# Encoder layer (attention, DeltaNet, experts): q, k, v projection of the DeltaNet as seven products of halves

## Chip, cores and metric

The kernel runs on one core of a Trainium2 chip. The metric is the device time of one execution in microseconds (us), the median over the runs. The engines are TensorE (PE, its weight loads PEld), VectorE (DVE), ScalarE (ACT), GpSimd (POOL) and SyncE (SP, which issues nearly all DMAs here).

## What is computed

One layer over two groups of tokens with the same weights, 256 prompt and 512 sample tokens, 768 in all (six tiles of 128; all float32, width 2048):

```
def encoder_layer(x, ...):
    h = rms_norm(x, norm1_g)
    proj = h @ w_in
    q_lat, kv_lat, k_rope, qkv, z, a_f, a_b, b_f, b_b = split_cols(proj, SPLITS)
    mla_out = mla_mixer(q_lat, kv_lat, k_rope, ...)          # 8 heads, softmax attention
    gdn_out = gdn_mixer(qkv, z, a_f, a_b, b_f, b_b, ...)     # 8 heads, DeltaNet
    x = x + jnp.concatenate([mla_out, gdn_out], axis=-1) @ w_o
    x = x + ec_moe(rms_norm(x, norm2_g), ...)
    return x
```

The change is about `qkv`: 3 types (q, k, v) x 8 heads x 128 columns of `w_in`, each a product of 768 tokens x 2048 with 2048 x 128, after which a convolution over five tokens and a SiLU follow.

## The kernel before

The work runs in five stages, each a function with a block of its own in which every engine has its own list of instructions; the order is written out by hand, and engines meet by semaphores alone.

- `latents` (to about 310 us): normalises and transposes the tokens into `xT` (all tokens, resident, 128 x 16 x 768), projects the latents of the attention, and the z columns by Strassen's scheme: the tokens' halves (first and second 1024 of the width, `a11`, `a12`, `a21`, `a22`) are paired by tiles through `Z_PAIRS`, VectorE forms sums of them (`form`, L478) in three buffers `zsum`, and weights' halves are summed in place. In their shade POOL forms the weight sums for `w_o`: 32 units, of each SP loads a piece (`comb_load`, L314), POOL subtracts three times (L591, L593, L595), SP stores the four results (`comb_store`, L323).
- `attention` (310 to 613 us): four groups of two heads. For every 128 queries `scores`, softmax on ScalarE and VectorE, `probs_t` (L913), `values`. TensorE is two units of scores ahead. Between them stand the projections of the next group (`project_mla`, L736 and L742). POOL does the rotation of the queries once a group (L1109 to L1122), after ScalarE has squared them; TensorE takes it at L891. VectorE copies each head's result to `mix_sb` (L1049) and SP stores that once a group (L850); the first copy of a group waits for the store of the group before. In the last group TensorE projects the first q/k/v tile (L943) and 8 steps of the second (L952) between its units. SP has little else here: the attention's weights (L838, L840).
- `deltanet` (613 to 1613 us): four passes, one per pair of heads. `project` (L1444 for the 512 sample columns, L1447 for the 256 of the prompt) makes 24 tiles, one for each type and head, with the 16 pieces of the width. Two tiles of the same type and pair are called a kind here; there are twelve. The first six tiles come first, the others inside the passes. A pass has three rounds of six levels (`round_`): TensorE multiplies (`product`, L1512), VectorE masks (L1916), TensorE multiplies (`back`, L1506), VectorE adds into `inv` (L1925) and transposes (L1911), ... ; between them stand the scans (L1539 to L1561) and, as fill, 3, 2 and 2 steps of projection a level (`IN_LEVEL`). ScalarE copies each tile from PSUM to `pre` (`copy_tile`, L1678, L1680); VectorE convolves those of k and q, POOL those of v (`convolve`, L2034, L2037). VectorE forms the output and its square sum (`output`, L1963), TensorE transposes it (L1571). In the last pass the fill is `partial`, the first part of the `w_o` product (L1587), for which SP first loads the mix (L1398), the first two parts of `w_o` (L1400) and the rest of the mix (L1402).
- `output_and_route` and `moe` (from 1613 us): the `w_o` product, the router and the experts. The change doesn't touch them but for a name.

## Time and profile before

| | |
|---|---|
| median of 3 runs | 2967.54 us (2966.45 to 2970.6) |
| the profiled execution | 2964.23 us, its span 2962.5 |
| mean granted TensorE clock | 0.980 of full speed |
| TensorE busy | 2797.9 us (94%) |
| VectorE, ScalarE, GpSimd busy | 1092.6, 611.1, 602.2 us |
| DMA | 603.95 MB, mean 204 GB/s |

A row of a timeline has the start in us from the span's start, the busy time, the engine, the line, the operation with output and inputs, the tile and the count, and in square brackets how long the engine was idle before, and who released it. A row of SP (SPq) is a DMA's issue and not its transfer. A float32 matmul leaves two records, so x32 stands for 16 matmuls.

### The profile page before, as it was taken

The page shows a single profiled execution, that of the slowest core. Times are in us where ns is not written, and L with a number is a line of the kernel's source. Part 1 is how long each engine was busy: PE and PEld are TensorE (multiplying, and loading weights), DVE is VectorE, ACT ScalarE, POOL GpSimd, SP SyncE. Part 2 cuts the span into 40 slices and gives each one's busy share as a digit, 9 for nine tenths or more (in the row PEclk, how much of TensorE's full clock was granted, in tenths as well). Part 3 has the DMA queues.
Part 4 walks back from the last instruction along what each step waited for, and adds up shares of the span by engine and source line. Part 5 has one row for each costly group of instructions (what it writes and reads, how often), then busy time and mean ns, then how long its engine had stood idle before and what let it go on. Part 6 is the DMA issues. An engine that isn't in the chain of part 4 may idle for free. (4 is left out here: it accounts for less than half of the span.)

```text
span 2962.5 us, 53948 instructions
## 1 busy us (share of the span) xinstructions
PE 2797.9 (94%) x19063; PEld 1395.3 (47%) x19063; DVE 1092.6 (37%) x2185; ACT 611.1 (21%) x1806; POOL 602.2 (20%) x969
## 2 busy tenths in 40 slices
PE   8999999999999999999788999999999999999997
PEld 4544455555666666567465445432223232322332
DVE  1145444421674575476675424411111111111100
ACT  4100455412213312321411011321111111111100
POOL 1444111104214222420530000211111111112111
PEclk9999999999999999999899999999999999999998
DMA  7663100021211110200413636799999999999996
GB/s 250 217 217 133 53 29 29 11 94 57 58 44 50 44 52 28 72 19 22 157 44 129 255 142 234 296 424 412 387 400 394 396 402 396 408 386 400 392 412 211
DMA packets 170388, 603.95 MB, mean 204 GB/s; under 512 B 16527, under 2 KB 81895, under 8 KB 116455
## 3 DMA queue, kind: packets, MB, share of 16 engines
q1 hardware_dynamic: 163175, 587.58, 51.4%
q0 software_dynamic: 6912, 12.59, 2.5%
q8 instruction: 161, 2.64, 0.4%
q14 instruction: 140, 1.15, 0.1%
HBM read 554.14 MB, written 45.98 MB: 203 GB/s over the span
## 5 line engine op out<-in xcount | busy, mean ns | idle before, releaser
L2727 PE MATMUL psum<-wbuf 128*32 128x512 f32 x2976 | 340.1, 610 | 24.7 <-issue 22.9
L1444 PE MATMUL psum<-xT,wbuf 128*128 128x512 f32 x720 | 340.9, 611 | 0.3 <-PEq L828 0.3
L2727 PE MATMUL psum<-x,wbuf 128*32 128x512 f32 x3024 | 330.1, 592 | 0.0
L715 POOL COPY wbuf<-xT 128x16 f32 x533 | 114.1, 214 | 775.1 <-issue 462.8
L715 DVE COPY wbuf<-xT 128x16 f32 x500 | 94.5, 190 | 337.5 <-issue 336.6
L2727 PEld LDWEIGHTS psum<-wbuf 128*32 128x32 f32 x2976 | 96.1, 113 | 252.4 <-issue 252.4
L2727 PEld LDWEIGHTS psum<-x,wbuf 128*32 128x32 f32 x3024 | 97.9, 110 | 226.6 <-issue 226.6
L1444 PEld LDWEIGHTS psum<-xT,wbuf 128*128 128x128 f32 x720 | 133.2, 194 | 126.9 <-issue 121.8
L2747 PE MATMUL psum<-x,hT 128*32 128x512 f32 x1584 | 172.9, 592 | 0.0
L715 ACT COPY wbuf<-xT 128x16 f32 x503 | 111.3, 221 | 275.7 <-issue 272.8
L2747 PE MATMUL psum<-wbuf,hT 128*32 128x512 f32 x1488 | 164.3, 597 | 2.0 <-DVE hT L2808 2.0
L1447 PE MATMUL psum<-xT,wbuf 128*128 128x256 f32 x736 | 164.9, 379 | 0.0
L1447 PEld LDWEIGHTS psum<-xT,wbuf 128*128 128x128 f32 x736 | 138.7, 190 | 25.5 <-issue 8.1
L2822 DVE TENSOR_SCALAR ye<-psum,gate 128x512 f32<-128x512 f32 x48 | 33.1, 745 | 302.5 <-PE psum L2747 302.5
L624 PE MATMUL psum<-wbuf,xT 128*128 128x512 f32 (+1 forms) x384 | 141.4, 526 | 0.9 <-DVE xT L453 0.9
L1512 PE MATMUL psum<-inv,mix_g 64*64 64x64 f32 (+1 forms) x2112 | 103.9, 230 | 38.4 <-DVE inv L1911 38.4
L1925 DVE TENSOR_TENSOR inv<-inv,psum 64x256 f32<-64x256 f32 (+1 forms) x264 | 116.9, 443 | 55.0 <-PE psum L1512 51.2
L1512 PEld LDWEIGHTS psum<-inv,mix_g 64*64 64x64 f32 (+1 forms) x2112 | 89.0, 141 | 94.5 <-DVE inv L1911 77.1
L1916 DVE TENSOR_TENSOR wbuf<-psum,blocks 128x512 f32<-128x512 f32 x144 | 96.7, 689 | 90.6 <-PE psum L1512 87.6
L2276 PE MATMUL psum<-wbuf,xT 128*128 128x512 f32 x260 | 121.8, 609 | 6.4 <-DVE x L2397 5.4
L2860 POOL DMA_INDIRECT out_y_sample<-ye,scatter_rows x32 | 49.9, 1559 | 378.6 <-DVE ye L2822 373.7
L2276 PE MATMUL psum<-wbuf 128*128 128x512 f32 x288 | 126.1, 594 | 0.0
(330 smaller groups left out, 3572.7 us busy)
## 6 DMA issues: line engine op xcount, KB each, us to landing
x<-in_w_down SPq DMA_DIRECT2D x66, 1024.0 KB, 11.0
wbuf<-in_w_gate SPq DMA_DIRECT2D x65, 1024.0 KB, 9.3
wbuf<-in_w_up SPq DMA_DIRECT2D x65, 1024.0 KB, 11.7
x<-in_w_gate SPq DMA_DIRECT2D x63, 1024.0 KB, 8.8
x<-in_w_up SPq DMA_DIRECT2D x63, 1024.0 KB, 11.2
wbuf<-in_w_down SPq DMA_DIRECT2D x62, 1024.0 KB, 11.2
wbuf<-in_w_in SPq DMA_DIRECT2D x16, 2048.0 KB, 8.7
wbuf<-weight_sums SPq DMA_DIRECT2D x16, 2048.0 KB, 9.1
```

What stands on the lines that cost most here:

```text
L624: last = nc.tensor.matmul(ps[:, u % 3, 0:n], xT[:, d, t * P:(t + 1) * P], wb[g % 2][:, d, 0:n], start=(d == 0), stop=(d == KD - 1))
L715: last = copy(k.xeT[:, half, :, t:t + 1], k.mixT[:, :, cols][:, :, bass.ds(r, 1)])
L1444: last = nc.tensor.matmul(ps[:, b, 0:SS_], wg[:, m % 2, d, h * P:(h + 1) * P], k.xT[:, d, SP_:T], start=(d == 0), stop=(d == KD - 1))
L1447: last = nc.tensor.matmul(ps[:, b + 1, 0:SP_], wg[:, m % 2, d, h * P:(h + 1) * P], k.xT[:, d, 0:SP_], start=(d == 0), stop=(d == KD - 1))
L1512: last = nc.tensor.matmul(ps[lo:hi, x, n * P + lo:n * P + hi], left[lo:hi, x, n, lo:hi], right[lo:hi, x, n, lo:hi], start=True, stop=True)
L1916: nc.vector.tensor_tensor(p1[:, x].rearrange("p (d h) c -> p d h c", d=2), ps[:, x, :].rearrange("p (d h c) -> p d h c", d=2, h=2), bcast( ...
L1925: last = nc.vector.tensor_tensor(o, o, bank[lo:hi, :, lo:hi], ALU.subtract)
L2276: last = nc.tensor.matmul(ps[:, u % 3, :], left, k.slot[v % 3][:, q, :], start=(q == 0), stop=(q == H - 1))
L2727: last = nc.tensor.matmul(ps[32 * j:32 * j + 32, g, :].rearrange("p (x n) -> p x n", x=2), xeT[:, half, q, 32 * g:32 * g + 32], m[:, :, kk ...
L2747: last = nc.tensor.matmul(ps[32 * j:32 * j + 32, 3 + g, :], hT[:, f, 32 * g:32 * g + 32], m[:, kk, 512 * j:512 * j + 512], start=(f == 0), ...
L2822: nc.vector.tensor_scalar(ye[:, g, :], ps[:, 3 + g, :], gate[:, g:g + 1], None, ALU.mult).then_inc(s_ye, 1)
L2860: nc.gpsimd.indirect_dma_start(y_s if 32 * g < CS else y_p, bass.IndirectOffsetOnAxis(ap=sq[:, g:g + 1], axis=0), ye[:, g, :], None, compu ...
```

## The change

Each kind is now a product of two by two blocks by Strassen's scheme. The tokens' halves (384 tokens each, `SIDE`) and the width's halves (8 pieces each, `HK`) give `A11`, `A12`, `A21`, `A22` with sums `S1` to `S4`; the weights' halves (width) and the two heads give the other factor, of which four sums are needed. Seven products of 8 matmuls with 384 columns take the place of 2 x 16 x (512 + 256) columns: 84 products, 672 matmuls.

- The token sums are those that z uses: `Z_PAIRS` is changed so that a pair is one tile of each half. They are stored to `token_operands` in DRAM from `zsum` (`sum_store`), and VectorE waits for that (`stored`) before it forms the next sum there. `A11`, `A12` are stored in the attention. `A22` stays in SBUF; the other six operands pass through three slots (`load_tokens`, 1.5 MB each), six loads a kind.
- The weight sums, 48 units of four loads, three POOL operations and one store, are made in the attention through three buffers (`load_to_combine`, `combine`, `comb_store`): 8 units before the first rotation, 16, 16 and 8 behind the next three. Weights of a product (0.5 MB) go through six slots (`load_weights`).
- VectorE adds six of a kind's seven products from PSUM into `pre` and `stay` (`add`, nine operations), ScalarE copies one (`keep`). ScalarE's two copies a tile are gone. There are two buffers `pre`.
- In the last group of the attention TensorE does 24 steps (before: 40 matmuls). The fill per level stays 3, 2 and 2 steps, each now of 384 columns. `output` is split: its squares are summed first, then two more products are added between the parts.
- In the last pass SP waits for the convolution of the last q and v kinds before it loads the second part of `w_o` (`convolved(sp, n)`).

```diff
-Z_PAIRS = ((0, 1), (2, 3), (4, 5))
+Z_PAIRS = ((0, 3), (1, 4), (2, 5))
...
+A11, A12, S1, S2, S3, S4, A22 = range(7)
+PRODUCT_ORDER = (1, 6, 2, 7, 5, 4, 3)
+TOKENS_OF = {1: A11, 2: A12, 3: S4, 4: A22, 5: S1, 6: S2, 7: S3}
+W_SLOTS = 6
+IN_ATTENTION = 3 * HK
...
+def load_to_combine(k, eng, u):
...
+    for g in range(2):
+        k0 = HK * g + 2 * kp
+        for h in range(2):
+            eng.dma_start(k.w_comb[u % COMB_BUFS][:, 2 * g + h], w[:, k0:k0 + 2, h * P:(h + 1) * P]).then_inc(k.s_cl[u % COMB_BUFS], 16)
...
+def product_step(k, p, d):
...
+    last = k.nc.tensor.matmul(k.psum[:, product_bank(p), 0:SIDE], k.w_slot[p % W_SLOTS][:, d, :],
+                              k.x_slot[v].rearrange("p (k t) -> p k t", k=HK)[:, d, :],
+                              start=(d == 0), stop=(d == HK - 1))
...
                     added()
+                    stored(i, 1)
                     form(i, a11[i], a21[i])
...
+                def comb_store(lo, hi):
+                    for u in range(lo, hi):
+                        n, kp = divmod(u, 4)
+                        x, before = u % COMB_BUFS, (u - 1) % COMB_BUFS
+                        sp.wait_ge(s_comb, comb_base + 3 * u + 3)
...
+                        sp.dma_start(k.wsum[n, :, :, 2 * P * kp:2 * P * (kp + 1)].rearrange("m p c -> p m c"),
+                                     w_comb[x].rearrange("p m k c -> p m (k c)")).then_inc(s_cs[x], 16)
+                        if u and u + 2 < N_COMB:
+                            sp.wait_ge(s_cs[before], cs_base[before] + 16 * ((u - 1) // COMB_BUFS + 1))
+                            load_to_combine(k, sp, u + 2)
...
+                comb_store(0, 6)
                 load_w(1)
+                comb_store(6, 12)
...
+                comb_store(12, 22)
+                load_w(2)
+                comb_store(22, 33)
                 for i in range(HP):
-                    if i + 2 < HP:
-                        load_w(i + 2)
+                    if i == 1:
+                        comb_store(33, 39)
+                        load_w(3)
+                        comb_store(39, N_COMB)
+                        for x in range(COMB_BUFS):
+                            sp.wait_ge(s_cs[x], cs_base[x] + 16 * N_COMB // COMB_BUFS)
+                        for p in (1, 2, 3):
+                            load_weights(k, sp, p)
+                        for v, o in ((0, A11), (1, A12)):
+                            sp.dma_start(k.tok[o], k.x_slot[v]).then_inc(k.s_tl[v], 16)
...
                     sp.wait_ge(s_mix, 4 * (i + 1))
...
+                combine(0, 8)
                 pool.wait_ge(s_c, 64)
...
+                    combine(*((8, 24), (24, 40), (40, N_COMB), (N_COMB, N_COMB))[i])
...
-                load_w(0, 1)
+                for p in (4, 5):
+                    load_weights(k, sp, p)
+                refill(0, 3)
...
                         for j in range(2):
+                            if j:
+                                for n in (KINDS - 2, KINDS - 1):
+                                    convolved(sp, n)
                             sp.dma_start(k.slot[j], weight_half(a, 0, 0, j)).then_inc(k.s_wo[j], 16)
...
-                project(0, 1, SECOND)
-                for c in range(2, NC):
-                    project(0, c)
+                project(21 * HK - IN_ATTENTION)
```

Three places in the order of instructions, each with the line, the operation with its output and inputs, and the semaphores that it waits for. First SP in the attention, before, from the weights of the second group to the end of the stage:

```order
L838 DMA wqkv<-in_w_q_b 128x4x384 [waits q_projected]
L840 DMA wqkv<-in_w_kv_b 128x2x512 [waits kv_projected]
L845 DMA z_gate<-pr 128x512 [waits last_z_added_or_gated] x3
L838 DMA wqkv<-in_w_q_b 128x4x384 [waits q_projected]
L840 DMA wqkv<-in_w_kv_b 128x2x512 [waits kv_projected]
L850 DMA mix<-mix_sb 128x2x768 [waits mla_mixed]
L838 DMA wqkv<-in_w_q_b 128x4x384 [waits q_projected]
L840 DMA wqkv<-in_w_kv_b 128x2x512 [waits kv_projected]
L850 DMA mix<-mix_sb 128x2x768 [waits mla_mixed] x3
```

And after, its end, where the names `token_sum_stored_then_tokens_loaded` are here the stores of the sums and of the tokens:

```order
L147 DMA wbuf<-in_w_in 128x2x128 [waits token_sum_stored_then_tokens_loaded2]
L147 DMA wbuf<-in_w_in 128x2x128 x3
L981 DMA qkv_weight_sums<-wbuf 128x4x256 [waits weights_combined] x2
L136 DMA wbuf<-qkv_weight_sums 128x1024 [waits token_sum_stored_then_tokens_loaded2,token_sum_stored_then_tokens_loaded1,token_sum_stored_then_tokens_loaded0]
L136 DMA wbuf<-in_w_in 128x8x128
L136 DMA wbuf<-qkv_weight_sums 128x1024
L1007 DMA token_operands<-xT 128x3072 x2
L1015 DMA mix<-mix_sb 128x2x768 [waits mla_mixed] x2
L152 DMA xT<-token_operands 128x3072 [waits token_sum_formed_then_qkv_product_done,token_sum_stored_then_tokens_loaded1,token_sum_stored_then_tokens_loaded0]
L1015 DMA mix<-mix_sb 128x2x768 [waits mla_mixed]
```

The second and third mix stores (L850, now L1015) stand behind all weight sums, three weights and both token stores; the first stands behind the 33rd.

POOL around a rotation (before L1109 to L1122, now L1282 to L1295). Before, rotation follows rotation:

```order
L1119 TENSOR_TENSOR wbuf<-qraw,rope 128x384 [waits mla_pool_step]
L1120 TENSOR_TENSOR wbuf<-qraw,rope 128x384
L1122 TENSOR_TENSOR qrot<-wbuf 128x12x32 [waits mla_pool_step]
L1109 TENSOR_TENSOR qraw<-qraw,gain 128x12x64 [waits mla_squared,q_rotated]
L1112 TENSOR_TENSOR wbuf<-qraw,rope 128x384 [waits mla_pool_step]
```

After, with the end of the eighth weight sum ahead of the first rotation and the ninth behind it:

```order
L1275 TENSOR_TENSOR wbuf<-wbuf 128x256 [waits weights_combined]
L1282 TENSOR_TENSOR qraw<-qraw,gain 128x12x64 [waits mla_squared,mla_constants]
L1285 TENSOR_TENSOR wbuf<-qraw,rope 128x384 [waits mla_pool_step]
L1286 TENSOR_TENSOR wbuf<-qraw,rope 128x384
L1290 TENSOR_TENSOR qrot<-wbuf 128x12x32 [waits mla_pool_step]
L1292 TENSOR_TENSOR wbuf<-qraw,rope 128x384 [waits mla_pool_step]
L1293 TENSOR_TENSOR wbuf<-qraw,rope 128x384
L1295 TENSOR_TENSOR qrot<-wbuf 128x12x32 [waits mla_pool_step]
L1271 TENSOR_TENSOR wbuf<-wbuf 128x512 [waits unit_loaded5,q_rotated]
L1273 TENSOR_TENSOR wbuf<-wbuf 128x256 [waits weights_combined]
L1275 TENSOR_TENSOR wbuf<-wbuf 128x256 [waits weights_combined]
```

Each rotation now waits for the sums ahead of it in POOL's list, and each sum for its four loads (`unit_loaded`).

SP in the last pass, before, from the store of the third pair's output:

```order
L1417 DMA mix<-mix_g 128x2x768 [waits output_stored]
L1398 DMA xT<-mix 128x8x768 [waits qkv_projected]
L1400 DMA wbuf<-in_w_o 128x8x512 x2
L1402 DMA xT<-mix 128x6x768 [waits deltanet_stored]
L1386 DMA rows<-gate_rows 128x512 [waits decayed_kq,lower_matrix]
L1386 DMA rows<-gate_rows 128x512
```

And after:

```order
L152 DMA xT<-token_operands 128x3072 [waits token_sum_formed_then_qkv_product_done] x2
L1613 DMA mix<-mix_g 128x2x768 [waits output_stored]
L1586 DMA xT<-mix 128x8x768 [waits token_sum_formed_then_qkv_product_done]
L1591 DMA wbuf<-in_w_o 128x8x512
L1591 DMA wbuf<-in_w_o 128x8x512 [waits v_convolve_step,kq_convolved]
L1593 DMA xT<-mix 128x6x768 [waits deltanet_stored]
L1572 DMA rows<-gate_rows 128x512 [waits decayed_kq,lower_matrix]
L1572 DMA rows<-gate_rows 128x512
```

A wait for the convolutions of q and v stands between the two loads of `w_o`, and the rest of the mix and the rows of the gates are behind it.

## Rows read from the trace of the kernel before

**Rows 1.** The page's busy times, share of the span and instructions.
```profile
PE 2797.9 (94%) x19063; PEld 1395.3 (47%) x19063; DVE 1092.6 (37%) x2185; ACT 611.1 (21%) x1806; POOL 602.2 (20%) x969
```

**Rows 2.** Timeline of TensorE, the q, k, v stream: start us, us busy, engine line op.
```profile
627.03 13.90 PE L1444 MATMUL psum<-xT,wbuf 128*128 128x512 f32 x32
640.76 7.07 PE L1447 MATMUL psum<-xT,wbuf 128*128 128x256 f32 x32
647.67 13.90 PE L1444 MATMUL psum<-xT,wbuf 128*128 128x512 f32 x32
```

**Rows 3.** Timeline of VectorE in a level of the rounds.
```profile
869.47 1.44 DVE L1916 TENSOR_TENSOR wbuf<-psum,blocks 128x512 f32<-128x512 f32 x2
871.92 0.85 DVE L1925 TENSOR_TENSOR inv<-inv,psum 64x256 f32<-64x256 f32 x2 [1.01 <-PE psum L1512]
...
875.18 1.44 DVE L1916 TENSOR_TENSOR wbuf<-psum,blocks 128x512 f32<-128x512 f32 x2
```

**Rows 4.** Timeline of TensorE in the same level.
```profile
869.50 0.68 PE L1512 MATMUL psum<-inv,mix_g 64*64 64x64 f32 x16 [0.75 <-DVE inv L1911]
```

**Rows 5.** Timeline of TensorE at the attention's first projections.
```profile
317.38 2.74 PE L736 MATMUL psum<-wqkv,qlT 128*128 128x384 f32 x8
319.96 1.88 PE L742 MATMUL psum<-wqkv,kvlT 128*128 128x512 f32 x4
```

**Rows 6.** Timeline of TensorE, last head group of the attention.
```profile
601.93 0.66 PE L913 MATMUL psum<-square,pr 128*128 128x128 f32 x4 [0.86 <-DVE pr L1040]
```

**Rows 7.** Timeline of TensorE, output of the third head pair, and first partial product.
```profile
1405.92 1.91 PE L1571 MATMUL psum<-square,wbuf 128*128 128x128 f32 x12 [2.76 <-DVE wbuf L1963]
...
1458.13 2.07 PE L1587 MATMUL psum<-wbuf,xT 128*128 128x512 f32 x2 [4.62 <-DMA xT<-mix]
```

**Rows 8.** Timeline of VectorE, copy of the mix, third group.
```profile
516.13 0.42 DVE L1049 COPY mix_sb<-psum 128x256 f32<-128x256 f32 x1
```

**Rows 9.** Timeline of SP, issues of DMAs, in the z projection.
```profile
168.41 4.72 SPq L314 DMA_DIRECT2D comb<-in_w_o  x2
```

**Rows 10.** Timeline of POOL, the sum that this load feeds.
```profile
182.73 1.26 POOL L591 TENSOR_TENSOR comb<-comb 128x512 f32<-128x512 f32 x1 [15.40 <-DMA comb<-in_w_o]
```

**Rows 11.** Timeline of VectorE, first of the S1 token sums.
```profile
178.41 1.23 DVE L478 TENSOR_TENSOR xs<-xT 128x1024 f32<-128x1024 f32 x1 [0.16 <-DVE zs L525]
```

**Rows 12.** Timeline of POOL, two weight sums for w_o.
```profile
114.41 1.27 POOL L591 TENSOR_TENSOR comb<-comb 128x512 f32<-128x512 f32 x1 [2.57 <-DMA comb<-in_w_o]
...
119.68 1.27 POOL L591 TENSOR_TENSOR comb<-comb 128x512 f32<-128x512 f32 x1 [2.39 <-DMA comb<-in_w_o]
```

**Rows 13.** Timeline of SP between them.
```profile
115.75 1.22 SPq L314 DMA_DIRECT2D comb<-in_w_o  x2
117.31 0.37 SPq L323 DMA_DIRECT2D weight_sums<-comb  x1
```

**Rows 14.** Timeline of POOL, query rotation of the second group.
```profile
400.58 1.82 POOL L1109 TENSOR_TENSOR qraw<-qraw,gain 128x768 f32<-128x768 f32 x1 [54.78 <-ACT wbuf L1137]
...
407.71 0.99 POOL L1122 TENSOR_TENSOR qrot<-wbuf 128x384 f32<-128x384 f32 x1
```

**Rows 15.** Timeline of TensorE where it takes the rotated queries.
```profile
416.91 0.55 PE L891 MATMUL psum<-square,qrot 128*128 128x128 f32 x3 [0.29 <-ACT krT L1175]
```

**Rows 16.** Windows: us, busy (x) of PE, PEld, DVE, ACT, POOL, PEclk, DMA share, GB/s.
```profile
614.00:622.00 8.00, 8.00 (x24) 4.33 (x23) 4.29 (x7) 4.29 (x6) 0.00 (x0) 1.00 1.00 325
2000.00:2010.00 10.00, 10.00 (x96) 2.99 (x92) 2.31 (x6) 2.99 (x14) 0.92 (x1) 1.00 1.01 426
```

**Rows 17.** Timeline of VectorE, one operation beside POOL's rotation and one without.
```profile
405.68 1.09 DVE L1040 TENSOR_SCALAR pr<-pr,wbuf 128x256 f32<-128x256 f32 x1
...
438.63 0.35 DVE L1040 TENSOR_SCALAR pr<-pr,wbuf 128x256 f32<-128x256 f32 x1
```

**Rows 18.** Groups of POOL by line: xcount | busy us, mean ns | idle before.
```profile
L2037 POOL TENSOR_TENSOR y<-y,qd 128x772 f32<-128x772 f32 x32 | 64.3, 2009 | 2.5
L2034 POOL TENSOR_TENSOR qd<-pre,convT 128x772 f32<-128x772 f32 x32 | 53.4, 1668 | 2.5
```

495 lines of the change are left out of this document (329 added, 166 removed).

## Prediction

> **What bounds the kernel now.** I read the totals first, then the stream of matmuls, then single stretches in order of time. TensorE is busy for 2797.9 of 2962.5 us [rows 1], so a saving of its columns shows in the end wherever TensorE is itself the late one. Outside the rounds it is: in the q, k, v stream 32 records (16 matmuls; each leaves two records) of 512 columns run from 627.03 to 640.76 and those of 256 to 647.67, with no gap [rows 2]. That is 20.64 us for a tile (one head's columns of one type), 0.858 us for a 512-column matmul and 0.432 for a 256-column one. Inside the rounds it is not: the mask operation of one level follows that of the level before by 875.18 - 869.47 = 5.71 us [rows 3], VectorE has no idle row between but a wait of 1.01 us for the product, and TensorE, with its fill done, idles 0.75 us for `inv` [rows 3, 4]. So what is cut from the fill of a level turns mostly into idle time.
>
> **The products.** A kind (two tiles) takes 41.28 us now. Afterwards it is 7 x 8 = 56 matmuls of 384 columns. The attention has such ones: 8 records from 317.38 to 319.96, 2.58 us or 0.645 us each [rows 5]. So 36.1 us for a kind, 5.2 less, 62 us over the twelve. What of it is real, place by place:
> - Last attention group: 40 matmuls (20.64 + 8 x 0.858 = 27.5 us) become 24 (15.5). That is 12.0 less; the softmax is just as late as TensorE there, with a wait of 0.86 us for `pr` [rows 6], and I take **-9**.
> - The rest of the first three kinds: 96.3 us become 144 x 0.645 = 92.9, **-3.4**.
> - Three passes over the rounds: each has 123.8 us of projection before and 108.4 after, but 8.1 of those 15.5 us lie in levels (18, 12 and 12 steps before and after). Outside: -7.3, three times -22. The squares of the output are now summed before the last additions, and more products stand ahead of the output's transposes, so their wait of 2.76 us [rows 7] goes: three times, less what is left of it, -7. Together **-29**. Of the last pass 2.4 us come behind its last round, where the end hangs on loads (below): **+2.4**.
>
> VectorE adds nine operations a kind, against six copies that ScalarE loses. They stand between levels and behind the rounds; I cost them at nothing: in the straight parts VectorE has room beside 36 us of matmuls, and in a level 1.01 us of waiting. If that cover fails, 81 additions in the passes of some 0.5 us (a copy of 256 columns takes 0.42, [rows 8]) would give +40 at the most; six tenths of them stand in straight parts, so I bound it at +16, for the range.
>
> **Token sums.** They exist already for z. Their first store stands in SP's queue behind the loads of z's weights; a load issued at 168.41 landed for its reader only by 182.73 [rows 9, 10], while VectorE forms the next sum in the same buffer at 178.41 [rows 11]. It now waits for the store: 4.3 us, with the issues of the other two stores **+4.8**. The three later stores have an empty queue.
>
> **Weight sums in the attention.** This decides. 48 combinations, each four loads, three POOL operations and a store, through three buffers, and SP and POOL both take them between other work: POOL the query rotations, SP the loads of attention weights and the mix stores. POOL did the like for w_o: from 114.41 to the store's issue at 117.31 it takes 2.9 us, and the two loads issued at 115.75 release it at 119.68, 3.9 us on [rows 12, 13]. Two issues take 1.22 us, so four take 2.4, and the load becomes 5.0 us. SP issues the load for combination u+2 behind the store of u (0.4 us), so two cycles hold 0.4 + 5.0 + 2.9: **4.1 us a combination**, where TensorE's pace allows less, as follows. POOL starts at about 310. Rotation 1 ends at 408.7 now (8.1 us, [rows 14]) and TensorE takes its result at 416.91 [rows 15]; with 24 combinations and one rotation ahead it ends at 310 + 98 + 16 = 424. All 48 and three rotations end at 310 + 197 + 24 = 531; overlap at each rotation (three buffers are then full) gives back some 8: 523. Only then does SP issue the last store (4 us to land), three weights (1.6 MB) and two token stores (3.1 MB), and behind these the second and third mix store. At the measured 325 GB/s [rows 16] the 5.5 MB up to and with the mix take 17 us, 14.5 if half goes at the higher rate: the mix lands at about 544.5. VectorE waits for that before it copies the next mix at 516.13 [rows 8]: 28 us late. Its softmax operations are queued behind that copy, and TensorE, with two units of scores ahead, runs dry soon after: **+27**, with the shift of rotation 1 inside it. The bounds: nothing if a combination takes at most ((516 - 18.5) - 310 - 24) / 48 = 3.4 us; and +50 if VectorE and POOL slow each other, as one VectorE operation of 256 columns does, 1.09 us beside a POOL operation and 0.35 without [rows 17]. 138 us of POOL work are new here, which makes either end thinkable; I take the middle, the cycle built from the nearest rows.
>
> The Trainium skill (SBUF — State Buffer, "Who interferes with whom") says that VectorE and GpSimd share one port pair as an exclusive lock, so POOL's new work costs VectorE; the pair of [rows 17] agrees in direction. It (DMA: Bandwidth & Descriptors, "Anatomy of one DMA") also fits a transfer as 2.0 us plus its bytes at 436 GB/s; by that a combination's load takes 4.4 us instead of 5.0.
>
> **Start of the products' stream.** Weights 4 and 5 are issued only after the attention, 6 with one token load behind product 0: 3.1 MB at 325 GB/s, 9.7 us and 0.4 of issue, while products 3 and what is left of 2 cover 5.2. **+4.9**. From there a kind needs six token loads (9.44 MB) and seven weights (3.67 MB), 13.1 MB in 36.1 us, 363 GB/s; the two rates seen are 325 and 426 [rows 16]. For the first kinds I add **+2.5**; in the rounds the fill is slow and the DMA has time.
>
> **Tail.** The last kinds' v convolution on POOL starts only when product 83 is added, for both heads, about 19 us behind the output's transposes at 1405.92, and is nine operations a head, five of 1.67 and four of 2.01 us, 33 us in all [rows 18]: it ends at +52. SP, which before issued the loads of w_o and the mix in a row when the projection was done, now waits for it ahead of the second half of w_o and the second mix load, 4.4 MB, 13.5 us at 325. TensorE's first partial product waits for just these: now at 1458.13, +52.2, with 4.62 us of idle [rows 7], then at about +64.7: **+12.5**.
>
> **Sum.** -9 - 3.4 - 29 + 2.4 + 4.8 + 27 + 4.9 + 2.5 + 12.5 = **+12.7**. The profiled execution took 2964.2 us (span 2962.5), so 2977; the median of the runs shown is 3.3 above it: **2980 us**. Its own range is 2970 to 2996.
>
> **Rivals.**
> - *POOL keeps pace* (other side). If the three buffers let loads and sums overlap so that a combination takes at most 3.4 us, the second mix store lands before 516 and the +27 goes: 2953. For it: POOL's own work is 2.9 us; the load could overlap wholly, as three buffers are one more than w_o's two. Against it: SP waits for the store behind each sum before it issues a load, four issues of it. It decides at 3.4 us.
> - *The lighter load.* A load of 4.4 us makes the cycle 3.8, the last sum comes 12 to 15 us sooner: about 2966. This is what the page's fit would give, and the rows only show loads of two issues.
> - *The stream is bound by DMA.* At 325 GB/s a kind takes 40.4 us, 4.3 more, in the first kinds (2.6 of them) and in the 1.5 kinds of each pass that stand straight, 7.1 kinds or 30.5 us, less the 2.5 taken: 3008. For it: pieces of 512 bytes in the weights; against it: the token loads have 12 KB in a row, and [rows 16] shows 426 for such.
> - *Levels pay too.* If TensorE were the bound in the rounds, 24 us more go: 2956. The rows of the level speak against it.
> - That the change does not reduce the matmuls is excluded by the order: 672 stand there.
>
> **Chances.** Forecast 0.45; POOL keeps pace 0.24; lighter load 0.13; DMA-bound 0.12; levels 0.06. No change is within 0.2%, 5.9 us, about what a measurement can tell here: 2961.6 to 2973.5. Faster: 0.24 + 0.05 from the levels = 0.29. Same: 0.11 from the lighter load and 0.03 of the forecast's low end = 0.14. Slower: the rest, 0.57. The range 2948 to 3010 takes in the rivals' own times and leaves out the ends of their spread and that of the bounds +50 and +16.
>
> **What would show it.** In the changed profile: in the rows of the sums a start-to-start distance near 4 us, the wait before each for its load, and not 3; the copy of the mix in the third group late by tens of us with TensorE idle behind it; the granted clock a little lower there. A gap of about 5 us at the products' start, the one wait of 4 to 5 us in front of the second token sum, TensorE's first partial product some 12 us further behind the output's transposes than 52.2, and per pass about 10 us less. Wrong if the mix copy in the third group follows its matmul at once, or if VectorE, with its new additions, stretches the levels beyond 5.7 us.

## The result and the profile after

The changed kernel takes 3018.07 us, the median of four runs (3010.51 to 3023.33), against 2969.07 us (2966.45 to 2970.67) for the one before: a ratio of 1.0165, with a 95% interval of 1.0151 to 1.018. That is 49 us slower. The forecast was 12 us slower, and the range ended at 3010. The profiled execution took 3010.51 us with a span of 3008.5, 46.0 more than the span before; all comparisons of places below are made between these two traces. One execution of tail_order and the profiled one of start_order ran in a slow state (5037 and 5997 us) and are left out of the medians of these two below.

The busy times of the page, to [rows 1]; the mean granted clock is 0.967, it was 0.980:

```profile
PE 2754.4 (92%) x18871; PEld 1371.3 (46%) x18871; DVE 1144.3 (38%) x2294; ACT 595.4 (20%) x1770; POOL 732.4 (24%) x1113
```

TensorE is busy for 43.5 us less, as it should be, and the span is longer: TensorE idles 90 us more. The columns alone had been priced at 62 us of busy time; where the other 18 us went, to the lower clock or elsewhere, isn't separated. The question is what TensorE waits for. Two kinds of places in the program can be found in both traces. First VectorE's copies of the mix, before:

```profile
386.85 0.42 DVE L1049 COPY mix_sb<-psum 128x256 f32<-128x256 f32 x1
...
451.50 0.42 DVE L1049 COPY mix_sb<-psum 128x256 f32<-128x256 f32 x1
...
607.77 0.69 DVE L1049 COPY mix_sb<-psum 128x512 f32<-128x512 f32 x1 [5.90 <-PE psum L925]
```

and after ([rows 8] is the third group's first copy before):

```profile
404.66 0.41 DVE L1209 COPY mix_sb<-psum 128x256 f32<-128x256 f32 x1
...
483.42 0.42 DVE L1209 COPY mix_sb<-psum 128x256 f32<-128x256 f32 x1 [7.35 <-DMA mix<-mix_sb]
...
567.51 0.42 DVE L1209 COPY mix_sb<-psum 128x256 f32<-128x256 f32 x1 [13.47 <-DMA mix<-mix_sb]
...
645.75 0.69 DVE L1209 COPY mix_sb<-psum 128x512 f32<-128x512 f32 x1 [5.48 <-PE psum L1090]
```

Then TensorE's transposes of each pair's output, before (the third is in [rows 7]):

```profile
928.78 2.61 PE L1571 MATMUL psum<-square,wbuf 128*128 128x128 f32 x12 [2.76 <-DVE wbuf L1963]
...
1166.77 1.71 PE L1571 MATMUL psum<-square,wbuf 128*128 128x128 f32 x12 [2.76 <-DVE wbuf L1963]
...
1613.33 1.47 PE L1571 MATMUL psum<-square,wbuf 128*128 128x128 f32 x12
```

and after:

```profile
969.59 1.53 PE L1767 MATMUL psum<-square,wbuf 128*128 128x128 f32 x12 [0.43 <-DVE wbuf L2171]
...
1198.27 1.53 PE L1767 MATMUL psum<-square,wbuf 128*128 128x128 f32 x12 [0.42 <-DVE wbuf L2171]
...
1428.70 1.53 PE L1767 MATMUL psum<-square,wbuf 128*128 128x128 f32 x12 [0.42 <-DVE wbuf L2171]
...
1662.97 1.48 PE L1767 MATMUL psum<-square,wbuf 128*128 128x128 f32 x12
```

The changed kernel is behind by 17.8 us at the first group's first copy, 31.9 and 51.4 at the two next groups', 38.0 at the last copy of the attention, 40.8, 31.5 and 22.8 at the three outputs, 49.6 at the last and 46.0 at the end. So 38 us are lost by the end of the attention, 7.5 of them by its first projections (one that starts at 320.48 started at 312.98 before), the second and third pass give 9 us each back, and the last pass loses 27.

**The levels.** They did what [rows 3, 4] said. One level after is 916.35 - 910.65 = 5.70 us, and the fill in it is 1.56 us where it was 1.98; the level is no shorter. After:

```profile
910.65 1.44 DVE L2121 TENSOR_TENSOR wbuf<-psum,blocks 128x512 f32<-128x512 f32 x2
...
916.35 1.44 DVE L2121 TENSOR_TENSOR wbuf<-psum,blocks 128x512 f32<-128x512 f32 x2
```

```profile
913.45 1.56 PE L158 MATMUL psum<-xT,wbuf 128*128 128x384 f32 x4
```

and the fill before:

```profile
872.27 1.98 PE L1444 MATMUL psum<-xT,wbuf 128*128 128x512 f32 x4
```

**The sums.** In the attention POOL starts a sum every 4.3 us, 407.20 - 398.57 = 8.63 us for two, and waits for a load at every second one:

```profile
398.57 1.27 POOL L1271 TENSOR_TENSOR wbuf<-wbuf 128x512 f32<-128x512 f32 x1 [2.70 <-DMA wbuf<-in_w_in]
...
407.20 1.27 POOL L1271 TENSOR_TENSOR wbuf<-wbuf 128x512 f32<-128x512 f32 x1 [2.74 <-DMA wbuf<-in_w_in]
```

```profile
392.94 0.37 SPq L981 DMA_DIRECT2D qkv_weight_sums<-wbuf  x1
...
393.36 2.64 SPq L147 DMA_DIRECT2D wbuf<-in_w_in  x4
...
401.47 0.37 SPq L981 DMA_DIRECT2D qkv_weight_sums<-wbuf  x1
```

The loop can be read from these: store at 392.94, four issues (2.64 us) from 393.36, POOL starts on them at 398.57, and the next store of that chain is at 401.47. That chain's cycle is 8.53 us, and it holds two sums.

**What stands behind them.** Besides the two waits for the mix store above (7.35 and 13.47 us) there are these. ScalarE may not overwrite `pr` before z is stored; the three stores are in SP's list behind the 12th sum. They went out at 381.78 where it was 353.67 before, and ScalarE, then TensorE wait (the profile names no releaser for ScalarE; with the stores moved ahead, in z_stores_8, this wait is gone):

```profile
381.78 1.45 SPq L993 DMA_DIRECT2D z_gate<-pr  x3
```

```profile
386.45 0.56 ACT L1357 ACTIVATE pr<-psum,wbuf,rsq 128x256 f32<-128x256 f32 x1 [12.94 <-issue]
```

```profile
387.75 0.69 PE L1078 MATMUL psum<-square,pr 128*128 128x128 f32 x2 [9.18 <-DVE pr L1200]
...
439.36 1.51 PE L1056 MATMUL psum<-square,qrot 128*128 128x128 f32 x6 [4.62 <-POOL qrot L1295]
...
515.23 1.51 PE L1056 MATMUL psum<-square,qrot 128*128 128x128 f32 x6 [7.26 <-POOL qrot L1295]
...
660.97 12.25 PE L158 MATMUL psum<-xT,wbuf 128*128 128x384 f32 x32 [5.10 <-DMA xT<-token_operands]
...
1448.56 2.04 PE L1654 MATMUL psum<-wbuf,ones 128*128 128x512 f32 x2 [9.15 <-ACT mix_g L1904]
...
1505.98 2.08 PE L1784 MATMUL psum<-wbuf,xT 128*128 128x512 f32 x2 [25.72 <-DMA xT<-mix]
```

The second and third of these six rows of TensorE are the rotations behind 24 and 40 sums, the fourth is the start of the products' stream. The fifth and sixth belong to the last pass. Behind the sixth, the wait for the mix, stand these rows of POOL and SP:

```profile
1458.18 2.06 POOL L2284 TENSOR_TENSOR y<-wbuf,convT 128x772 f32<-128x772 f32 x1 [52.72 <-DVE wbuf L2062]
...
1490.06 1.81 POOL L2287 TENSOR_TENSOR y<-y,qd 128x772 f32<-128x772 f32 x1
```

```profile
1491.94 0.37 SPq L1591 DMA_DIRECT2D wbuf<-in_w_o  x1
...
1492.35 0.58 SPq L1593 DMA_DIRECT2D xT<-mix  x1
```

POOL convolves v from 1458.18 to 1491.9, only then does SP issue the rest, and TensorE starts on the mix 14 us later.

### The profile page after: what moved, and what is told of

The parts are those of the page before. It is cut to its first block and busy times, and to the rows that moved or that the text cites. A ratio compares the mean times of both kernels' runs of the same rounds, so it can differ in the third digit from the quotient of the medians.

```text
span 3008.5 us, 54407 instructions
## 1 busy us (share of the span) xinstructions
PE 2754.4 (92%) x18871; PEld 1371.3 (46%) x18871; DVE 1144.3 (38%) x2294; ACT 595.4 (20%) x1770; POOL 732.4 (24%) x1113
## 5 line engine op out<-in xcount | busy, mean ns | idle before, releaser
L158 PE MATMUL psum<-xT,wbuf 128*128 128x384 f32 x1344 | 472.0, 499 | 8.5 <-DMA xT<-token_operands 5.1
L158 PEld LDWEIGHTS psum<-xT,wbuf 128*128 128x128 f32 x1344 | 252.4, 194 | 165.2 <-issue 21.7
L2319 POOL TENSOR_TENSOR tf<-inv,b_col 128x256 f32<-128x256 f32 x48 | 30.2, 660 | 368.9 <-DVE inv L2130 368.9
L1708 PE MATMUL psum<-inv,wbuf 64*64 64x64 f32 (+1 forms) x2112 | 97.7, 234 | 11.3 <-DVE wbuf L2121 10.7
```

The lines of the kernel that those rows point to most:

```text
L158: last = k.nc.tensor.matmul(k.psum[:, product_bank(p), 0:SIDE], k.w_slot[p % W_SLOTS][:, d, :], k.x_slot[v].rearrange("p (k t) -> p k t", ...
L1708: last = nc.tensor.matmul(ps[lo:hi, x, n * P + lo:n * P + hi], left[lo:hi, x, n, lo:hi], right[lo:hi, x, n, lo:hi], start=True, stop=True)
L2319: last = nc.gpsimd.tensor_tensor(tf[:, x, two], tt[:, x, two], bcast(bv[:, d, 2 * i:2 * i + 2, tiles[d]], 2, P), ALU.mult)
```

## Experiments

Theory A: the sums' chain is slow by itself and harmless, but SP and POOL take their lists in order, and mix stores, z stores, attention weights and rotations are queued behind sums; the same holds for the mix load behind the last convolutions. Theory B, the rival: the additional work itself (POOL beside VectorE, DMA traffic, VectorE's additions) takes the time, wherever it stands. All experiments start from the changed kernel and are compared with the kernel before on the same chip. Times are medians. The kernel before has medians of 2967.46 to 2969.24 us beside them, and the changed kernel's four executions spread over 13 us, so a difference of a few us from its 3018.07 is no evidence by itself; there the places in the traces decide.

### tail_order: the second mix load ahead of the wait

```diff
-                        for j in range(2):
-                            if j:
-                                for n in (KINDS - 2, KINDS - 1):
-                                    convolved(sp, n)
-                            sp.dma_start(k.slot[j], weight_half(a, 0, 0, j)).then_inc(k.s_wo[j], 16)
+                        sp.dma_start(k.slot[0], weight_half(a, 0, 0, 0)).then_inc(k.s_wo[0], 16)
                         sp.wait_ge(s_out, i * 16)
                         sp.dma_start(k.mixT[:, H:2 * H - 2], k.mix[H:2 * H - 2].rearrange("h p t -> p h t")).then_inc(k.s_mix, 16)
+                        for n in (KINDS - 2, KINDS - 1):
+                            convolved(sp, n)
+                        sp.dma_start(k.slot[1], weight_half(a, 0, 0, 1)).then_inc(k.s_wo[1], 16)
```

> Edit: in the last pass SP issues the second mix load ahead of the wait for the last convolutions; only the second part of w_o stays behind that wait. Theory A (the wait between the two w_o loads costs the tail): from the output's transposes to TensorE's first partial product it is 77.3 us in the changed kernel, 52.2 before; here the two mix loads and the first part of w_o, 7.5 MB, land some 20 us after the last product, so about 51 us, and the run is 26 us shorter: about 2992. Rival B (the late products and the late v convolution on GpSimd hold the first round by themselves): the first partial product moves, but the mask operations behind it wait for GpSimd's factors, and the run gains under 10 us: above 3008.

2994.51 us, ratio 1.0096 (1.0075 to 1.0117): 24 us less than the changed kernel. The first partial product has no wait any more; it follows the output (here at 1427.52) by 51.6 us:

```profile
1479.12 2.08 PE L1783 MATMUL psum<-wbuf,xT 128*128 128x512 f32 x2
```

Theory A holds: the load queued behind the late convolution was what cost. What the convolution costs by itself is at most 4 us: from the third to the last output it is 211.7 us here, 234.3 in the changed kernel and 207.4 in the one before.

### mix_first: the mix stores ahead of the last sums

```diff
-                comb_store(22, 33)
+                comb_store(22, 30)
+                sp.wait_ge(s_mix, 4)
+                sp.dma_start(k.mix[0:2].rearrange("h p t -> p h t"), mix_sb[:]).then_inc(s_out, 16)
+                comb_store(30, 39)
...
+                comb_store(39, 46)
+                sp.wait_ge(s_mix, 8)
+                sp.dma_start(k.mix[2:4].rearrange("h p t -> p h t"), mix_sb[:]).then_inc(s_out, 16)
```

> Edit: SP stores the first mix behind the 30th weight sum (before: 33rd) and the second behind the 46th, ahead of the remaining sums, the weights and the token stores. Theory A: VectorE's waits for the mix store, 7.35 and 13.47 us, go; but the rotation of the third group still waits for 40 sums, so the first of them is eaten by it and the gain is 13 us: 3005. Rival B (the two waits are the whole delay of the attention behind its first group): 21 us or more, 2997 or less. Rival C (sums are late anyway and something else takes the place at the second too): no change, 3018.

3007.02 us, 1.0139 (1.0121 to 1.0157): 11 us less. The last copy is at 634.51 instead of 645.75. As A says, only the second wait is gained; at the first, the rotation behind 40 sums takes over (TensorE's wait for it is 9.32 us, it was 7.26). The third group's first copy is at 552.81, still 36.7 us later than before the change: the mix store wasn't alone.

### few_sums: 12 sums instead of 48

```diff
-N_COMB = 4 * KINDS
+N_COMB = 12
...
-        src = k.wsum[n, SUMS_OF[q]].rearrange("p (k c) -> p k c", c=P)
+        src = k.wsum[n % 3, SUMS_OF[q]].rearrange("p (k c) -> p k c", c=P)
```

> Edit: only the 12 weight sums of the first three kinds are made; the others' loads, operations and stores are left out, and their products read the first three kinds' sums, so the output of the other heads is not the reference's. Theory A (the sums' pace delays the attention): the attention's last mix copy comes at about 612 instead of 646, since only the late first token sum and the first rotation (together 16 us less the 12 of the lighter fill) are left, and the run takes 34 us less, 2984. Rival B (the fill and the token transfers are at fault, not the sums): under 10 us less, above 3008.

2981.12 us, 1.0042 (1.0027 to 1.0056): 37 us less, and the last copy is at 611.98, both as theory A had them. The run leaves out 36 sums, and most products read sums that aren't theirs; what TensorE has to do is the same.

```profile
611.98 0.69 DVE L1206 COPY mix_sb<-psum 128x512 f32<-128x512 f32 x1 [5.48 <-PE psum L1087]
```

So three quarters of the loss are the sums' chain with what stands behind it. Whether as order or as contention, this run doesn't tell; a comparison of windows helps. From the first copy of a group's second head to the next copy the same matmuls run (74 to 81 records in these four; columns as in [rows 16]). Before, in few_sums (with no sums left), and in rot_and_weights and all_moved_4 below (with sums):

```profile
414.81:438.89 24.08, 21.75 (x77) 12.03 (x76) 8.63 (x26) 9.22 (x29) 0.00 (x0) 1.00 0.00 1
```

```profile
428.88:452.96 24.08, 21.75 (x77) 12.03 (x76) 8.64 (x26) 9.24 (x29) 0.00 (x0) 1.00 0.00 1
```

```profile
433.35:461.49 28.14, 24.82 (x81) 13.81 (x80) 12.02 (x27) 10.09 (x33) 17.69 (x19) 0.94 0.84 247
```

```profile
495.96:519.78 23.82, 21.27 (x74) 11.65 (x73) 10.05 (x27) 9.16 (x29) 14.28 (x16) 1.00 0.85 247
```

24.08 us, 24.08, 28.14 and 23.82. VectorE's busy time for the same work rises from 8.63 to 12.02 us beside 17.69 us of POOL, and the granted clock falls to 0.94. That is the longest of the stretches with sums and no wait for a rotation or a store: three others take 25.52 (rot_and_weights), 25.27 and 26.39 (all_moved_2), and the last one shown loses nothing although VectorE is busy for 10.05 us in it. So part of B is real, but it costs between nothing and 4 us in such a stretch, and in the longest one a part of the 4 is the clock. The Trainium skill (SBUF — State Buffer, "Who interferes with whom") has a reason for VectorE's longer operations, a port pair that VectorE and GpSimd lock in turn. The windows agree in direction, but the sums' DMA traffic is there at the same time, and no run separates the two.

### s4_early: the first token sum's stores ahead of the weights

```diff
-                comb_store(13, 18)
-                load_w(3)
-                sum_store(S4, 0)
+                comb_store(13, 16)
+                sum_store(S4, 0)
+                comb_store(16, 18)
+                load_w(3)
```

> Edit: the three stores of the first token sum are issued two weight sums earlier, ahead of the load of z's last weights. Theory A (the store behind 4 MB of weights makes VectorE wait 4.47 us): the wait goes and TensorE's wait for g_col is again about 5.6 us instead of 10.25; 4.6 us less, 3013. Rival B (the store only shifts the wait to the weight sums and loads behind it): no gain, 3018.

3015.99 us, 1.016 (1.0136 to 1.0185), which can't be told from the changed kernel's. In the trace the wait went, from

```profile
184.71 1.23 DVE L600 TENSOR_TENSOR xs<-xT 128x1024 f32<-128x1024 f32 x1 [4.47 <-DMA token_operands<-xs]
```

```profile
201.01 0.45 PE L815 MATMUL psum<-square,g_col 128*96 128x128 f32 x1 [10.25 <-DVE g_col L655]
```

to a wait of 6.16 us for g_col, and the first mix copy is 4.9 us earlier (399.76):

```profile
197.05 0.45 PE L816 MATMUL psum<-square,g_col 128*96 128x128 f32 x1 [6.16 <-DVE g_col L656]
```

Its last copy is only 3.8 us earlier: the second mix store's wait grew from 13.47 to 15.98 us.

### rot_earlier, load_ahead, all_moved: two misses

rot_earlier puts 6, 13, 13, 13 and 3 sums around the rotations. The mix stores are moved as in mix_first, to behind the 29th and 44th sum, which is not shown here.

```diff
-                combine(0, 8)
+                combine(0, 6)
...
-                    combine(*((8, 24), (24, 40), (40, N_COMB), (N_COMB, N_COMB))[i])
+                    combine(*((6, 19), (19, 32), (32, 45), (45, N_COMB))[i])
```

> Edit: as mix_first (mix stores now behind the 29th and 44th sum), and the sums around the rotations are 6, 13, 13, 13 and 3 instead of 8, 16, 16 and 8, so that the sums' list runs into the last group. Theory A (48 sums of 4.3 us each are harmless once nothing of the attention is queued behind them): the rotations come in time, the last mix copy is at about 613, as with few_sums, and the run takes about 2985. Rival B (VectorE and GpSimd slow each other while sums run, and sums take DMA from the attention): the last mix copy stays above 622 and the run above 2993.

3037.39 us, 1.0229 (1.0211 to 1.0247): 19 us more. Theory A missed, and B's bounds (above 622 and above 2993) are met, but not by B's cause. TensorE waited for the attention's weights, which SP loads behind the 22nd and 39th sum, and these now come later:

```profile
449.26 4.97 PE L861 MATMUL psum<-wqkv,qlT 128*128 128x384 f32 x8 [11.54 <-DMA wqkv<-in_w_kv_b]
...
544.79 4.99 PE L861 MATMUL psum<-wqkv,qlT 128*128 128x384 f32 x8 [27.27 <-DMA wqkv<-in_w_kv_b]
```

It is theory A's mechanism, at a load that I had left where it was.

load_ahead issues a sum's load ahead of the wait for the sum before it:

```diff
+                        if u and u + 2 < N_COMB:
+                            sp.wait_ge(s_cs[before], cs_base[before] + 16 * ((u - 1) // COMB_BUFS + 1))
+                            load_to_combine(k, sp, u + 2)
                         sp.wait_ge(s_comb, comb_base + 3 * u + 3)
...
-                        if u and u + 2 < N_COMB:
-                            sp.wait_ge(s_cs[before], cs_base[before] + 16 * ((u - 1) // COMB_BUFS + 1))
-                            load_to_combine(k, sp, u + 2)
```

> Edit: SP issues the load of weight sum u+2 as soon as the store of sum u-1 has landed, ahead of its wait for sum u. Theory A (the cycle of two sums is store, four issues, landing, operations; with this edit it becomes the cycle of one buffer, 0.4 + 3.6 + 5.2 + 2.9 = 12.1 us for three sums): the distance falls from 4.27 to 4.03 us, the last sum comes 10 us earlier and with it the second mix store; the run takes 8 to 11 us less, 3008. Rival B (DMA bandwidth sets the pace): distance unchanged, 3018.

3051.44 us, 1.0284 (1.0267 to 1.0301): 33 us more. SP's rows tell why:

```profile
382.11 1.91 SPq L147 DMA_DIRECT2D wbuf<-in_w_in  x4
...
384.05 0.47 SPq L984 DMA_DIRECT2D qkv_weight_sums<-wbuf  x1
...
387.28 1.91 SPq L147 DMA_DIRECT2D wbuf<-in_w_in  x4
...
389.23 0.47 SPq L984 DMA_DIRECT2D qkv_weight_sums<-wbuf  x1
```

Each store is now held by the wait for the store before it and by four issues: 0.47 + 2.76 + 1.91 us, one sum every 5.2 us. I had worked out the cycle of a buffer and left out that SP serves all three in one list. It confirms how sensitive the attention is to the sums' pace: 0.9 us more a sum made the last copy of the attention (680.04 against 645.75) 34 us later. all_moved held both of these with tail_order, s4_early and conv_first.

> Edit: tail_order, s4_early, rot_earlier, load_ahead and conv_first together. Theory A (the waits are independent and each is a matter of order): 3018 - 33 - 4.6 - 22 - 4 = 2954, below the kernel before by 13 us. Rival B (the DMA traffic and the additional VectorE work eat the fewer columns): 2967 or more.

3017.05 us, 1.0159 (1.0142 to 1.0176). It says little, since both misses are in it: its attention ends at 671.78, 26 us later than the changed kernel's, and what tail_order and conv_first gain behind it makes up for that.

### conv_first: a convolution ahead of an addition

```diff
-                        add(p0 + 19)
                         convolve(i + 1, 3)
+                        add(p0 + 19)
```

> Edit: VectorE does the convolution of the second q tile ahead of the addition of the product before the last, instead of behind it. Theory A (in the last pass TensorE's wait of 9.15 us for the third sum of squares hangs on this convolution, 4.4 us late): the wait falls to about 4.7 us, product 83 and all behind it come 4 us sooner; 3014. Rival B (the additions' order doesn't matter): 3018, or more, where the late addition holds a product.

3012.03 us, 1.0146 (1.0129 to 1.0163): 6 us less, which is within the changed kernel's spread. By the places it is about 4: TensorE's wait for the third sum of squares in the last pass fell from 9.15 us to

```profile
1447.27 2.04 PE L1654 MATMUL psum<-wbuf,ones 128*128 128x512 f32 x2 [4.79 <-ACT mix_g L1904]
```

and from the third output's transposes to the last's it is 229.8 us instead of 234.3.

### rot_and_weights, moved_without_rot, all_moved_2

rot_and_weights, against rot_earlier:

```diff
-                comb_store(12, 22)
+                comb_store(12, 18)
                 load_w(2)
-                comb_store(22, 29)
+                comb_store(18, 29)
...
-                comb_store(29, 39)
+                comb_store(29, 31)
                 load_w(3)
-                comb_store(39, 44)
+                comb_store(31, 44)
```

> Edit: as rot_earlier, and the attention's weights of the third and fourth group are loaded behind the 18th and 31st sum instead of the 22nd and 39th. rot_earlier was 20 us slower, with TensorE waiting 11.54 and 27.27 us for just these weights, which stood behind sums that now come later. Theory A (the sums are harmless once nothing that the attention needs is queued behind them): both waits go, the last mix copy is at about 613, and the run takes about 2985. Rival B (VectorE and GpSimd slow each other while sums run): above 2993.

3010.73 us, 1.0142 (1.0127 to 1.0157): 27 us less than rot_earlier, so the weights were its fault, but it is not 2985. Its last copy is at 641.20 instead of A's 613, and the time is in B's range. The second mix store now stands behind the 44th sum, which comes later too, and that wait is about half of these 28 us; the run alone doesn't settle what the other half is:

```profile
553.63 0.43 DVE L1214 COPY mix_sb<-psum 128x256 f32<-128x256 f32 x1 [14.97 <-DMA mix<-mix_sb]
```

The next two have no edits of their own: they join those above.

> Edit: tail_order, s4_early, mix_first and conv_first together; the sums around the rotations stay 8, 16, 16 and 8. Theory A: 3018 - 11 - 4 - 22 - 5 = 2976, slower than the kernel before by 0.3%, since the rotations still wait for the sums ahead of them. Rival B (the waits overlap): above 2985.

2973.18 us, 1.0018 (1.0006 to 1.0029), from ten executions between 2965.64 and 2980.4. A's sum was 2976, B had above 2985.

> Edit: tail_order, s4_early, rot_and_weights and conv_first together (load_ahead, which lost, left out). Theory A (each wait is a matter of order, and they add up): 3018 - 33 - 4 - 22 - 5 = 2954, 0.45% below the kernel before. Rival B (traffic and additions eat the fewer columns): 2967 or more.

2978.43 us, 1.0032 (1.0018 to 1.0046), from twelve between 2965.17 and 2989.93. A's 2954 missed by 24, and the time is in B's range again (2967 or more), with waits of A's kind in the trace: the mix stores waited 2.66 and 11.32 us again, and the last group 5.91 us for product weights that stand behind the last sums.

### z_stores_8, start_order, all_moved_4

```diff
-                comb_store(6, 12)
+                comb_store(6, 8)
...
-                comb_store(12, 22)
+                comb_store(8, 22)
```

> Edit: the three stores of z (SP's list, behind the 12th sum, issued at 381.78 us where the values were ready at 362.8) come behind the 8th sum. ScalarE waits for them before its first softmax (12.94 us of idle, TensorE 9.18 us for pr). Theory A (several things are queued behind the same chain of sums, and the latest of them sets the pace): the first mix copy comes 10 us sooner, at 395, but the rotation of the second group still stands behind 24 sums, so TensorE's wait of 4.6 us there grows to 14 and the run gains at most 2 us: 3017. Rival B (the delays add up): the run gains the 10 us, 3008.

3013.55 us, 1.0155 (1.0135 to 1.0176): 4.5 us less, within the two kernels' spread. The three stores go out at 359.87, ScalarE has no wait for them, the first copy is at 395.85, 8.8 us earlier, and the rotation behind 24 sums takes most of it, 11.93 us instead of 4.62:

```profile
437.58 1.51 PE L1056 MATMUL psum<-square,qrot 128*128 128x128 f32 x6 [11.93 <-POOL qrot L1295]
```

start_order issues two loads within the attention:

```diff
+                        load_weights(k, sp, 6)
+                        sp.wait_ge(k.s_prod, PROD_BASE + 2)
+                        for v, o in TOKEN_LOADS[1]:
+                            load_tokens(k, sp, v, o)
+                        load_weights(k, sp, 7)
...
-                refill(0, 3)
+                refill(2, 3)
```

> Edit: the token load behind product 1 and the weights of products 6 and 7 are issued within the attention, as soon as product 1 is done, instead of in the next stage, where product 4 waits 5.10 us for that token load. Theory A (a wait of order): the 5.1 us go; 3013. Rival B (the stream is bound by DMA there at 360 to 376 GB/s): the wait moves to the next products, under 2 us gained, 3017.

3006.97 us, 1.0143 (1.0122 to 1.0164), 11 us less. With 3013 and 3017 the theories are closer to each other than the changed kernel's executions are, so the time doesn't decide between them, and the trace of this run can't be set beside the others. all_moved_4, which has this edit, decides it: its stream has no wait for tokens and none of over 3 us, and from the last mix copy to the first sums of squares it takes 106.4 us, against 111.5 in all_moved_2, 112.0 in the changed kernel and 107.0 in the one before. The 5 us were a matter of order.

all_moved_4 joins these and places the list anew, against all_moved_2:

```diff
-                combine(0, 6)
+                combine(0, 4)
...
-                    combine(*((6, 19), (19, 32), (32, 45), (45, N_COMB))[i])
+                    combine(*((4, 20), (20, 33), (33, N_COMB), (N_COMB, N_COMB))[i])
...
-                comb_store(18, 29)
+                comb_store(18, 27)
                 sp.wait_ge(s_mix, 4)
...
-                comb_store(31, 44)
+                comb_store(31, 39)
                 sp.wait_ge(s_mix, 8)
```

> Edit: tail_order, s4_early, conv_first, start_order, the z stores behind the 8th sum, the mix stores behind the 27th and 39th, the attention's weights behind the 18th and 31st, and 4, 16, 13 and 15 sums ahead of the four rotations. all_moved_2 still waited 2.66 and 11.32 us for mix stores, 5.91 for weight sums in the last group and 5.57 for tokens at the start. Theory A (nothing of the attention is queued behind a sum that comes later): 2978 - 14 - 6 - 5 - 5 = 2950, below the kernel before by 0.6%. Rival B (GpSimd's and VectorE's overlap and the traffic cost what is left): 2960 or more.

2953.65 us (2951.47 to 2956.53), ratio 0.9955 (0.994 to 0.9971): 14.5 us faster than the kernel before and 64 faster than the changed one. Same 84 products, same 48 sums, same bytes; only the order of issue is another. The third output's transposes are at 1400.71 (before 1405.92, [rows 7]), and the last copy is this:

```profile
615.48 0.69 DVE L1220 COPY mix_sb<-psum 128x512 f32<-128x512 f32 x1 [5.47 <-PE psum L1101]
```

The attention still ends 7.7 us later than before (607.77). The first part of that is again a load behind sums. The attention's weights are issued at 359.08, behind the sixth sum, where it was 334.76 before, and TensorE waits for them and is slow behind the wait:

```profile
366.30 4.54 PE L862 MATMUL psum<-wqkv,qlT 128*128 128x384 f32 x8 [3.12 <-DMA wqkv<-in_w_kv_b]
```

Ahead of it the kernel is 3.8 us late, behind it 8.0, and still 8.0 at the first copy (394.86), though the sums run beside it all that time. Over the wait of 4.00 us for the second group's rotation it becomes 15.1, at the first group's last copy (453.95); the second and third group add 2.5 more, and the last group, with its lighter fill, gives 10 back.

## Why the prediction was wrong

The sign was forecast, and so were the places in the attention and in the last pass. The wait at the token sums, the start of the stream and the second and third pass came out within about 1 us. The step that failed is the price of what waits behind the weight sums in the attention, and with it the start of the tail: both mechanisms were there, and both were priced far too low. The size was off by 33 us of the profiled span (46.0 against 12.7): 2.7 ahead of the attention, 12.5 in it, 1.1 at the start, 8.9 in the passes and 12.0 in the last, less 3.6 behind it. By the steps of the sum:

- **Token sums**, +4.8: 4.6 by TensorE's wait for g_col (10.25 less 5.64). Another 2.9 us of delay stand in this stage by 320 us; 2.0 of them were there already at 167 us, and their cause stays open.
- **Weight sums**, +27 with -9 in the last group, so +18: between 320 us and the last copy 30.5. The mechanism held: pace, rotations, second mix store. Taken apart, the +27 is at the third group's first copy, which is 51.4 us late, 7.5 of it from the stage before: 43.9 where 27 were forecast. Of that 3.5 us come back with the next copy, and the last group gives back 9.9 for the forecast 9. Three sizes were wrong. A sum took 4.3 us and not 4.1: the load is 5.2 us from first issue and not 5.0, and the prediction's own 8.3 us for two sums are 4.15 and not 4.1. Over 48 that is 8 us. The list began at 318 and not 310, since the stage before it had become longer, which the sum had in another line and didn't carry over. And the 8 us of overlap that I subtracted "at each rotation" didn't exist to that extent. The last sum ended at 546.7 instead of 523, and the mix landed at 567.5 instead of 544.5. And the forecast looked at this one wait alone: mix_first, without it, is still 36.7 us late at that copy, by the stage before, the z stores and the rotations.
- **A queue left out.** The z stores behind the 12th sum stand in the diff, and the prediction doesn't name them. They cost about 9 us at the first copy: so much earlier it is in z_stores_8. That run also shows that alone they matter little, because the rotation behind 24 sums caught up. In all_moved_4 they are moved along with the rest.
- **Contention**, in the prediction only as a bound (+50 with both mechanisms): between nothing and 4 us in a stretch of 24 us of attention, by the windows above. How much of the changed kernel's loss it is, no run shows; in all_moved_4, which has sums beside the attention all through its second group, the lateness grows by 2.5 us over the second and third group, where TensorE has no wait of over 2 us.
- **Start of the stream**, +4.9 and +2.5, less 3.4: from the last copy to the first sums of squares 112.0 us against 107.0, +5.1 for +4.0. The wait for product 4 was 5.10 us. That the cause is order and not bandwidth, all_moved_4 shows with 106.4 us.
- **Levels don't pay; passes**, -9.7 each: -9.3 and -8.7 for the second and third. The first gave only -2.2 by the landmarks. Of the missing 7.5 us 5.2 are an error of the sum, which takes the whole saving of three passes up to the third output: before, 10 matmuls of 512 and 16 of 256 columns stood behind it, 15.5 us, and now 16 of 384, 10.3 us, so this part of the saving lies behind the output, where the tail's price has it already. The other 2.3 stay open.
- **Additions at nothing**: held in the levels (5.70 us). It failed in one place: the addition of the product before the last stands between two convolutions and waits 3.81 us for its product. That is half of TensorE's wait of 9.15 us, and worth about 4 us by the places in conv_first.
- **Tail**, +12.5 and +2.4: the last pass lost 26.9. The convolution's 33 us and the load's 14 were right. The start was wrong: product 83 was added 29.5 us behind the output's transposes, and I took 19. I had counted the matmuls behind the output and not the sums of squares that stand among them and wait for ScalarE.
- **The clock**, written down as "a little lower" and priced at nothing: what it cost in all isn't separated; the last section has two places.

Of the rivals, none is what happened. "POOL keeps pace" fell at once with a pace of 4.3 us, the lighter load with 5.2 us from issue to use, and that the levels pay too with 5.70 us a level. (The fit that the prediction takes from the Trainium skill, DMA: Bandwidth & Descriptors, "Anatomy of one DMA", is one for DMAs that GpSimd issues; these are SyncE's.) The rival of a stream bound by DMA had a time of 3008, near the result, for a wrong reason: the stream's waits are 5.10 us and two short ones.

The forecast's own range, 2970 to 2996, was too narrow because it held the places of the queue at fixed times. With one list as the bound, errors of pace and of start didn't average out here; the pace counted 48 times, and with the start and the missing overlap it made the last sum 24 us later than forecast.

## What to carry to other kernels

Fewer columns on the engine that is busy 94% of the time gained 43 us of busy time and lost 90 us to waits. Most of these were entries of an in-order queue that stood behind a slow chain without needing it: all_moved_4, where only the order differs, idles 58 us less than the changed kernel. When a change adds a long chain to a queue, go through every entry of that queue behind it and write down when it was issued before, who needs it, and when it will be issued now; then place each at its due time. And after each move, do it again for the next entry: moving the rotations made the weights late, and moving these left the mix stores late.

## What the runs showed of the hardware

- The clock made waits cost a second time. In the gap of 9.15 us ahead of 1448.56 TensorE idles; from 1448.6 to 1452.0 it runs at a granted clock of 0.50 of full speed, which is the lower of the two levels, 1.2 of 2.4 GHz. Before the gap it had 1.00. The third row is conv_first, where the gap is 4.79 us:

```profile
1434.00:1439.00 5.00, 5.00 (x18) 2.92 (x16) 1.19 (x3) 0.94 (x2) 0.00 (x0) 1.00 0.04 14
...
1448.60:1452.00 3.40, 3.40 (x6) 1.89 (x7) 1.76 (x2) 2.83 (x5) 0.00 (x0) 0.50 0.00 0
...
1447.30:1452.00 4.70, 4.70 (x8) 2.58 (x9) 1.77 (x2) 4.10 (x7) 0.00 (x0) 0.50 0.00 0
```

  The five matmuls at 1451.25 took 4.2 us instead of the 3.2 that five of 0.645 us take. Halving the gap didn't save that: in conv_first the matmuls behind the gap are at 0.50 for no shorter a time, and the same five took 4.7 us. In the attention's windows the clock was 0.88 (345 to 400 us, 0.97 before) and 0.89 (515 to 560, 1.00 before).
- Of one kernel's executions the longer have the lower clock: 3010.51 us at 0.967 and 3023.33 at 0.961 for the changed one, 2965.17 at 0.975 and 2989.93 at 0.965 for all_moved_2. Which is the cause of the other isn't shown. How far executions spread doesn't follow how much a kernel waits: 13 us in four for the changed kernel, 3 in four for conv_first, 25 in twelve for all_moved_2, 5 in six for all_moved_4.
- A load of 512 KB in four issues took 2.6 us to issue and 5.2 us to be usable, against 1.2 and 3.9 for two issues of the same bytes [rows 12, 13]. The pieces were of 512 bytes instead of 1 KB, too, and the runs don't tell the two apart.
